# First unit, memory norm and residual norms by token half in a two-block float32 transformer kernel

## The reference

```
mem_n = rms_norm(mem, mem_norm_g)                  # 256 memory rows of 1024
h = rms_norm(x, g_mix_pre[i]);  proj = h @ w_in[i]
tok = mixer(q, k, v)                               # layer 0 banded, layer 1 full attention
mkv = mem_n @ w_mem_kv[i];  mo = memory_attention(qm, km, vm)
o = concatenate([tok, mo]) @ w_o[i]
x = x + rms_norm(o, g_mix_post[i])
h = rms_norm(x, g_ffn_pre[i]);  gu = h @ w_gate_up[i]
f = (silu(gu[..., :D_FF]) * gu[..., D_FF:]) @ w_down[i]
x = x + rms_norm(f, g_ffn_post[i])
```

## Time and profile before

| | us |
|---|---|
| median of 3 runs | 1735.75 |
| lowest, highest | 1733.74, 1735.92 |
| the profiled execution | 1735.17 |
| span of the profiled execution (first to last instruction) | 1733.0 |

### The profile page before, as it was taken

The page is one execution under the profiler, slowest core; times in us unless marked ns, Lnnn a source line. Parts: engine busy times, 40 slices in busy tenths (PEclk is TensorE's granted clock), DMA queues, the critical chain, the costliest instruction groups (busy, mean ns, idle before and its releaser), DMA issues.

```text
span 1733.0 us, 25057 instructions
## 1 busy us (share of the span) xinstructions
PE 1642.1 (95%) x9953; PEld 1407.3 (81%) x9953; DVE 1091.1 (63%) x1384; ACT 877.8 (51%) x1308; POOL 55.7 (3%) x102
## 2 busy tenths in 40 slices
PE   4989999998999989999998999999999999899997
PEld 4968888895888878888976788888888897688886
DVE  3776565677666666565656566657565656656654
ACT  4455444465544455444645454445444554554443
POOL 1000000020000002000000000002000000000000
PEclk8999999999999999999998999999999998999999
DMA  7504555541455557555540245556655541045551
GB/s 228 171 27 146 202 185 194 182 147 32 151 194 194 183 193 212 197 176 194 159 133 1 76 168 192 188 197 200 208 181 194 168 148 50 1 148 197 190 194 72
DMA packets 211150, 271.73 MB, mean 157 GB/s; under 512 B 4824, under 2 KB 191824, under 8 KB 211072
## 3 DMA queue, kind: packets, MB, share of 16 engines
q1 hardware_dynamic: 208528, 263.56, 45.7%
q0 software_dynamic: 2544, 7.09, 1.7%
HBM read 269.58 MB, written 1.05 MB: 156 GB/s over the span
## 4 chain that ended last, share of the span: by engine, by line
PE 87%; DVE 7%; ACT 3%; issue 1%; DMA 1%; SPq 0%; POOL 0%; DVEq 0%; POOLq 0%; ACTq 0%
PE pair L1681 29%; PE pair L1683 14%; PE bank L1638 12%; PE bank L1640 12%; PE bank L1639 12%; PE bank L1809 1%; PE pair L1790 1%; PE pair L1628 1%; DVE probs L1150 1%; ACT probs L779 1%; DMA raw<-in_w_mem_kv 1%; PE bank L1839 1%; DVE negmax L1114 1%; PE bank L1756 1%; DVE w_lo L984 1%
## 5 line engine op out<-in xcount | busy, mean ns | idle before, releaser
L1681 PE MATMUL pair<-xt,w_hi 128*128 128x512 f32 x2112 | 750.0, 399 | 1.4 <-DVE xt L993 1.4
L984 DVE TENSOR_TENSOR w_lo<-raw,w_hi 128x2048 fp32r<-128x2048 f32 x248 | 567.9, 2290 | 160.8 <-ACT w_hi L657 158.9
L657 ACT ACTIVATE w_hi<-raw 128x2048 fp32r<-128x2048 f32 x248 | 474.1, 1914 | 294.3 <-PE pair L1683 201.0
L1683 PE MATMUL pair<-xt,w_lo 128*128 128x256 f32 x2112 | 592.7, 281 | 0.0
L1681 PEld LDWEIGHTS pair<-xt,w_hi 128*128 128x128 f32 x2112 | 397.3, 188 | 99.9 <-issue 2.2
L1683 PEld LDWEIGHTS pair<-xt,w_lo 128*128 128x128 f32 x2112 | 399.3, 189 | 2.3
L1638 PE MATMUL bank<-w_hi,xt 128*128 128x256 f32 x736 | 210.7, 286 | 0.4 <-DVE xt L993 0.4
L1640 PE MATMUL bank<-w_lo,xt 128*128 128x256 f32 x736 | 208.2, 283 | 0.0
L1639 PE MATMUL bank<-w_hi,xt 128*128 128x256 f32 x736 | 208.2, 283 | 0.0
L1638 PE MATMUL bank<-w_hi,hid_hi 128*128 128x512 f32 x528 | 207.3, 393 | 0.0
L1640 PE MATMUL bank<-w_lo,hid_hi 128*128 128x512 f32 x528 | 206.4, 391 | 0.0
(11 more groups left out here) (242 smaller groups left out, 1423.3 us busy)
## 6 DMA issues: line engine op xcount, KB each, us to landing
raw<-in_w_gate_up SPq DMA_DIRECT2D x44, 1024.0 KB, 5.1
raw<-in_ffn_wg SPq DMA_DIRECT2D x44, 1024.0 KB, 5.1
raw<-in_ffn_wu SPq DMA_DIRECT2D x44, 1024.0 KB, 5.1
raw<-in_ffn_wd SPq DMA_DIRECT2D x44, 1024.0 KB, 5.0
raw<-in_w_in SPq DMA_DIRECT2D x30, 1024.0 KB, 5.3
raw<-in_w_down SPq DMA_DIRECT2D x22, 1024.0 KB, 5.0
raw<-in_w_o SPq DMA_DIRECT2D x8, 1024.0 KB, 5.2
raw<-in_w_out SPq DMA_DIRECT2D x8, 1024.0 KB, 5.3
```

Source lines behind the costliest of these rows:

```text
L657: act.activation(w_hi[s][:, :], raw[s][:, :], ACT.Copy).then_inc(hi_ready, 1)
L984: dve.tensor_tensor(w_lo[s][:, :], raw[s][:, :], w_hi[s][:, :].bitcast(F32), ALU.subtract)\
L1681: pe.matmul(out[:, 512 * m:512 * (m + 1)], w[0][:, c, cols], xt[:, 2 * SEQ * c:2 * SEQ * (c + 1)], start=(c == 0), stop=False)
L1683: last = pe.matmul(out[:, 512 * m + SEQ:512 * (m + 1)], w[1][:, c, cols], hi_half(xt, c), start=False, stop=(c == KC - 1))
```

## The change

- Opening: SP loads constants, then the memory, then the weights. The memory's gain row, the other gain rows and the masks are issued by ACT. The first two post-norm gains are issued by POOL after the memory's norm. PE turns the memory's gain rows alone first (8 rows), and all 88 after unit 0, before x; DVE copies them and ACT's and DVE's work on x waits for that copy. ACT runs a one-column copy first and makes the memory's high halves before those of units 0 and 1; DVE does the same with the low halves. The masks are copied after that.
- Unit 0 (`first_unit`): for the first token half all high-by-high products, then all low-by-high ones, then those with the unit's low half, each group behind its own wait; then the same for the second half.
- Output projections of the first block: the fourth unit's first token half goes to bank 3 and is announced by itself (`o_half`). Squares, sum, rstd, gain and four additions are made per token half. The split of the first up unit moves on DVE behind the low halves of the turned x. PE turns x by token half (`turn_halves`).
- Feed-forwards of the first block: the last down unit runs t outside, b inside; squares, sum, rstd and additions per token half.
- Second layer's memory product: its first unit goes to bank 3 without waiting for DVE's scaling, then x is turned by halves (the fourth piece waits until ACT has copied that unit), then the second unit waits for the scaling.

The diff, cut to its core:

```diff
@@ sync
             sp.dma_start(cst[:, :], a["constants"][:, 0:C_W]).then_inc(consts_landed, 16)
-            at = 0
-            for src in gain_rows:
-                n = src.shape[0]
-                sp.dma_start(proj_at[at:at + n, 512:640], src).then_inc(rows_landed, 16)
-                at += n
             sp.dma_start(h, a["mem"][0].rearrange("(t p) n -> p t n", p=P)).then_inc(mem_landed, 16)
-            sp.dma_start(proj_at[:, 0:2 * P], a["constants"][:, C_UP:]).then_inc(consts_landed, 16)
@@ gpsimd
-            load_gain(0)
-            load_gain(1)
+            def norm_halves(j):
+                c = norm_column(j)
+                for t in range(NT):
+                    power([(c + t, c + t + 1, D)], ("norm", j, t), head_squares)
             norm(0)
+            load_gain(0)
+            load_gain(1)
...
-                norm(2 + 4 * l, head_squares)
+                norm_halves(2 + 4 * l)
@@ scalar, opening
+            act.dma_start(proj_at[0:8, 512:640], gain_rows[0]).then_inc(mem_gain_landed, 16)
+            for src in gain_rows[1:]:
+                act.dma_start(proj_at[at:at + n, 512:640], src).then_inc(rows_landed, 16)
+            act.dma_start(proj_at[:, 0:2 * P], a["constants"][:, C_UP:]).then_inc(masks_landed, 16)
+            act.wait_ge(pool_order.sem, pool_order.at("ones"))
+            act.activation(rowsum[:, 0:1], ones[:, 0:1], ACT.Copy)
+            act.wait_ge(prep_ready.sem, prep_ready.at("gains_t"))
+            turn_hi("mem", 0, memt)
             split_hi(0)
             split_hi(1)
-            act.wait_ge(prep_ready.sem, prep_ready.at("gains_t"))
-            turn_hi("mem", 0, memt)
             squares_of(h, 0)
@@ scalar, out_projection
                     if norm:
-                        act.wait_ge(unit_used, u0 + k + 1)
                         for t in range(NT):
+                            if k == 3 and t == 0:
+                                act.wait_ge(o_half, l + 1)
+                            else:
+                                act.wait_ge(unit_used, u0 + k + 1)
@@ vector
+            turn_lo("mem", 0, memt)
             split_lo(0)
             split_lo(1)
-            turn_lo("mem", 0, memt)
...
+                if l == 0:
+                    dve.wait_ge(small_mm.sem, small_mm.at("all gains_t"))
+                    link(dve.tensor_copy(gains_t[:, 8:88], ACC[1][:, 8:88]), prep_ready, "all gains_t")
                 split_lo(u + 2)
...
+                for t in range(NT):
+                    dve.wait_ge(squares.sem, squares.at(("piece", l, 3, t)))
+                    sum_squares(4, 2 + 4 * l, t)
+                    link(dve.tensor_tensor(osm[:, t, 768:1024], (ACC[3] if t else bank[3])[:, 256 * t:256 * (t + 1)],
+                                           gain[0][:, 768:1024], ALU.mult), prep_ready, ("osum", l))
+                    add_norm(2 + 4 * l, ("ffn", l), t)
+                turn_lo(("ffn", l), 3 + 4 * l)
+                split_lo(u + 3 + AHEAD)
...
+                dve.wait_ge(squares.sem, squares.at(("half", l, 0, 0)))
+                scaled(0, 0)
+                dve.wait_ge(squares.sem, squares.at(("half", l, 0, 1)))
+                sum_squares(2, 4 + 4 * l, 0)
+                scaled(0, 1)
+                add_norm(4 + 4 * l, following, 0)
+                dve.wait_ge(squares.sem, squares.at(("half", l, 1, 1)))
+                sum_squares(2, 4 + 4 * l, 1)
+                scaled(1, 0)
+                scaled(1, 1)
+                add_norm(4 + 4 * l, following, 1)
@@ tensor
+            def turn_halves(name, freed=None):
+                for t in range(NT):
+                    for p in range(4):
+                        pe.wait_ge(prep_ready.sem, prep_ready.at(("rows", name, p, t)))
+                        if freed and t == 0 and p == 3:
+                            pe.wait_ge(proj_out.sem, proj_out.at(freed))
+                        for e in range(2):
+                            c = 2 * p + e
+                            last = pe.transpose(TURN[p][:, SEQ * e + P * t:SEQ * e + P * (t + 1)],
+                                                x[:, t, P * c:P * (c + 1)], ident)
+                        if t:
+                            last.then_inc(turned.sem, turned.mark((name, p)))
...
+            def turn_first():
+                pe.wait_ge(rows_landed, 16 * (len(gain_rows) - 1))
+                pe.transpose(ACC[1][:, 0:88], proj_at[0:88, 512:640], ident[0:88, 0:88])\
+                  .then_inc(small_mm.sem, small_mm.mark("all gains_t"))
+                turn(("mix", 0), x, x_landed)
...
-                    pe.wait_ge(prep_ready.sem, prep_ready.at(("fsum", l - 1)))
-                projection(u, 2, 2, memt, pieces="mem" if l == 0 else None,
-                           before={1: lambda: turn(("mix", l), x, None if l else x_landed)})
+                if l == 0:
+                    projection(u, 2, 2, memt, pieces="mem", before={1: turn_first})
+                else:
+                    pe.wait_ge(up_summed, NG)
+                    projection(u, 1, 3, memt, banks=bank[0:4])
+                    turn_halves(("mix", l), ("unit", u))
+                    pe.wait_ge(prep_ready.sem, prep_ready.at(("fsum", l - 1)))
+                    projection(u + 1, 1, 3, memt)
...
-                    for b in range(2):
-                        for t in range(NT):
+                    for i1 in range(2):
+                        for i2 in range(NT):
+                            t, b = (i1, i2) if last_group and f < 2 else (i2, i1)
```

More of the change, by code:

```diff
@@ L606, in _ @@
                 norm(3 + 4 * l)
[L607 removed]
+                norm_halves(4 + 4 * l)
                 load_gain(2 + 2 * l)
@@ L858, in _ @@
                         act.wait_ge(half_used, l + 1)
-                    for t in range(NT):
+                    for b in range(2):
                         c = 16 + 2 * t + b
@@ L1660, in projection @@
                                 pe.wait_ge(turned_lo.sem, turned_lo.at((pieces, c // 2)))
-                            last = three(ACC[(k0 + k) % 4][:, 256 * t:256 * (t + 1)],
+                            out = bank[3] if half and k == n - 1 and t == 0 else (banks or ACC)[(k0 + k) % 4]
+                            last = three(out[:, 256 * t:256 * (t + 1)],
                                          xt_chunk(t, hi_half(src, c)), xt_chunk(t, lo_half(src, c)),
@@ L1664, in projection @@
                                          c == order[0], c == order[-1])
+                        if half and k == n - 1 and t == 0:
+                            last.then_inc(half, 1)
                     last.then_inc(unit_used, 1)
@@ L1897, in _ @@
             for l in range(2):
-                turn(("ffn1", l))
+                if l:
+                    turn(("ffn1", l))
+                else:
+                    turn_halves(("ffn1", l))
                 ffn(2 + 2 * l, ("ffn1", l))
```

131 lines of the change are left out of this document (78 added, 53 removed).

## The result

The changed kernel took 1715.49 us (median of four runs, 1714.12 to 1716.64), the kernel before, beside it, 1735.64 us (four runs, 1733.74 to 1735.92): ratio 0.9886, 95% interval 0.9869 to 0.9903. That is 20.2 us faster; 1716.2 us was forecast. On another chip the pair was measured again: 1716.25 us (1715.21 to 1716.39) against 1733.05 us (seven runs), ratio 0.9903 (0.9887 to 0.9920), 16.8 us. The profiled executions are 1735.17 us (span 1733.0) and 1716.06 us (span 1714.3).

The account below looks back on a forecast made before the run. TensorE, busy 95% of the span, was taken as the bound, with gains only where it idles or runs at half clock. -10.7 - 1.7 - 4.8 - 1.7 - 0.6 = -19.5 us from the median 1735.75 gave 1716.2 us, range 1709.5 to 1722.5.

Parts of the forecast that it names:

- A: Opening: the first product of unit 0 starts near 15.2 us instead of 26.13; -10.7 us, ends -8.0 and -13.0.
- The term for the broadcasts: Opening: taking POOL's 1.05 MB of gain broadcasts out of the early traffic brings the loads 2.7 us earlier.
- The term for the rows' issue: Opening: gain rows off SP move the memory's start by 2.63 us, of which 2.0 us were counted as gained.
- the full engines at 8 GB/s: Opening: DMA engines were full with 8 GB/s in the fifth microsecond, read as small packets that stay.
- R2: Rival, opening: small packets hold the engines until 8 us, memory lands at 12.0, gain only 8.0 us; 1718.9 us, chance 0.12.
- B: End of layer 1's output projection: token halves hide four additions under the last unit; -1.7 us.
- D: End of layer 2's output projection: the same string by token halves; -1.7 us.
- R3: Rival: the token halves give nothing at the output projections and the second feed-forward's end; 1720.2 us, chance 0.08.
- C: End of the first feed-forward: the next memory product starts without waiting for VectorE; -4.8 us, ends -3.8 and -5.3.
- E: End of the second feed-forward: token halves, VectorE's own work fills the string; -0.6 us, ends +0.3 and -1.7.
- R1: Rival: less idleness brings the clock up earlier, unit 0 -2.3 us and 0.6 at two ends; 1712.7 us, chance 0.15.
- R4: Rival: gain rows or masks from ScalarE's queue land late and stall TensorE; landing at 47 us gives 1739.3, chance 0.02.

Follow-up runs that it names:

- e2: The changed kernel, but POOL issues the two 0.5 MB broadcasts of gains at the start again; 1718.26 us.
- e3: The changed kernel, but SP issues the gain rows ahead of the memory and the masks behind it again; 1715.02 us.
- e9: The changed kernel, but POOL asks for its three small tables only after the memory's norm; 1712.24 us, beside 1716.25 for the changed kernel.
- e7: The changed kernel with both output projections' ends whole and the first up unit's split ahead of the sum, as before; 1718.67 us.
- e4: The changed kernel, but SP waits for the memory's landing before it issues weight unit 1; 1715.81 us.
- e5: The changed kernel, but the second layer's first memory product waits again until VectorE has scaled all four banks; 1720.96 us.
- e6: The changed kernel with the end of the second layer's feed-forward whole again (both token halves together); 1715.15 us.
- e1: The changed kernel with the opening of the kernel before (loads, order of halves, one turn of all gain rows); 1726.4 us.
- e8: The changed kernel with unread products filling TensorE's pauses at both output projections' ends and the second feed-forward's end; 1713.03 us.
- e10: The changed kernel with both the three small tables after the memory's norm and the unread products in TensorE's pauses; 1709.86 us.

## Why the prediction was right, and where it was not

*A, -10.7 forecast, -11.05 measured: the size right, two terms wrong against each other.* The memory was forecast at 9.3 us and landed at 6.7; unit 0 was forecast at 13.2 and landed at 13.4. I had let the memory's string (turn, high halves until 13.2) and unit 0 end together, so the one that was 2.6 us better hid behind the other. The term for the broadcasts was 2.7 us for both loads; e2 shows 2.2 for unit 0. The term for the rows' issue was 2.0; e3 shows 0.7 in the end. What is left, 7 to 9 us, I put down to the order (the memory's high halves before the units' and the first product on one unit only) and the landings that it leans on; no run took the order alone away. The step that I got wrong was the full engines at 8 GB/s. I read them as a loss that stays (R2) and never asked whose packets they were. They were POOL's tables (102.2% of the engines in that microsecond), and e9 moves those three loads for 2.0 us at the first product. R2 itself (memory at 12.0) didn't come.

*B and D, -1.7 each: the string right, the clock not priced.* The first feed-forward product starts 1.82 us earlier than the earlier trace rows less the shift by then (132.48 against 146.72 - 12.42), in D 1.80 us. e7 takes the halves away, and the string is back at 6.57 and 6.56 us, so R3 is refuted. But B gives -0.9 to -1.05 in five profiles (the changed kernel's first, e2, e4, e5, e6) and -1.9 in three (its second, e3, e9): the five have a stretch of half clock between 132 and 138 us, which costs 1 us, and the three have none; e1, with one twice as long (141 to 149), has +0.53. The kernel before has it too, in both profiles (144 to 149, 140 to 148). Whether one comes differs between executions of one kernel. D is the same: -1.65 in the changed kernel's first profile, without half clock there, and -0.47 in its second, with it.

*C, -4.8: right.* Measured -4.43, no gap, clock 1.00 throughout, a pause of 0.37 us in the turn for ScalarE's copy where 0.5 was forecast. e5 shows the wait as its cause.

*E, -0.6: the string right, the sign of the stage wrong.* The first product is at 628.70, 0.50 us earlier than 648.89 less 19.69. The first half's squares, sum and additions did run as counted, VectorE with 0.2 us of pause from 617.98 to 627.1. What I left out was TensorE: in the earlier trace rows's layout it had one pause and then the turn and the products in one piece, now three pauses in 6 us, and the clock that fell in them gave back 2.15 us (1.65 + 0.50) in the first profile and 1.5 in the second. The kernel before had its half clock at this end too, 6.8 us long in both profiles, but most of it lay over the pause and the turn: it ended 1.2 and 1.4 us after the first product, where in the nine profiles with halves and no fills it ended 3.1 to 6.0 us after it. e8 and e10 (pauses filled, -1.28 and -1.27) show that the clock was the loss; e6 (one pause, -0.47, half clock for 0.3 us behind the first product) fits, but is one profile.

*R1, the clock comes up earlier,* was half right at best. Unit 0 took 7.88 us in the first profile of the changed kernel and 7.12 in the second, for 8.50 and 8.24 in the two of before; but e1, with the old opening, took 7.11. Of the 0.6 us each that I gave it in B and E nothing came: at E the clock went the other way, at B it differs from profile to profile. By the Trainium skill ("TensorE: Matmul & The Clock Gate", Part 1) the throttled state is the default and activity releases it. At E the runs agree (with the pauses filled the clock stayed at 1.00); in the opening e1 doesn't bear it out as a price for idleness, with 7.2 us of it before unit 0 and 7.11 for the unit.

*R4* was far off: the masks, the last of ScalarE's loads, had landed by 13.8 us (issued at 4.48, 9.3 us to landing), and VectorE read them at 21.2.

The sum of the forecast holds in total (-19.5 against -18.7 and -19.0 of span) because A's surplus, the attention's chance and E's loss cancel; that the total came so close is in part luck. The medians, -20.2 on one chip and -16.8 on the other, leave both open.

## What to carry to other kernels

Where DMA engines are busy and move little, look up whose packets they are: small tables (71 KB here, 6 of them the worst), asked for early and needed late, can hold back the megabyte that everything waits for. A norm by token half pays by what it hides under the last unit, but count TensorE's pauses as well as the string: with three short ones the half clock lay over products, with one long one mostly over the pause, and unread products in them gave 1.5 to 2.9 us in that stage here (-1.28 against +0.19 to +1.65). Ask what each of two strings would be without the other; when they end together, gaining on one alone gives nothing.

## What the runs showed of the hardware

- POOL's 96 packets took 0.36 us of an engine each, SP's 0.075 (the queue table of e9's section); the sink's 16 of 384 bytes took 1.29 us each in the changed kernel and 1.12 in the kernel before. Size alone doesn't order them: POOL's of 4096 bytes took 0.50 us, SP's 0.20. Why is left open. Without them the engines moved 358 GB/s in the ninth microsecond, with them 234 and 96.
- Holding the megabyte behind it back until 6.34 us (e4) did not bring unit 0 earlier: high half at 14.17, 13.43 without the hold.
- TensorE's pace follows the record of the granted clock, but the record has a first entry, and before it the windows print 1.00. In the eleven profiles with the new opening that entry comes between 9.9 and 21.0 us. In seven of them it comes after the first product of unit 0 (the changed kernel's second profile 18.5, e9 19.1, e10 19.2, e2 21.0), and there the products before it are 0.21 us apart and those behind it 0.12: they ran at half pace although the window prints 1.00. In the other four the pace changes with the record's rows (the changed kernel's first profile: half until 20.3; e3: full from 17.1, half from 18.0 to 21.4). Half pace ended between 18.5 and 20.3 us in the changed kernel, e9 and e10, though the first product lay between 13.0 and 15.6: what is started earlier there is partly given back.
- At E the clock fell to one half among pauses of only 1.30, 1.72 and 0.5 to 0.7 us in all nine profiles with the halves and no fills, and lost 3.4 to 5.1 us (counted as above; with one pause of 4.5 us it lost 1.7 in e6 and 3.4 in both profiles of the kernel before). What a stretch costs depends on how much of it lies over products. With the pauses filled (0.23 us left ahead of the first turn) it stayed at 1.00 in e8 and e10.
